# Two blocks of a network on one core: filler matmuls in TensorE's waits, and the values of two dilated heads in one step

## The reference

```
aff = softmax(h @ w_router);  vals, idx = top_k(aff^T, 32)      # per expert
hid = silu(xs @ w_gate) * (xs @ w_up);  y = (hid @ w_down) * vals
out[idx] += y
```

```
for (window, dilation) in ((128, 1), (512, 4), (2048, 16)):     # three configurations of every dilated head
    o, lse = attention(q, k, v, offsets 0, dilation, 2*dilation, ... up to window)
out = sum(softmax(lse over the three) * o)
```

## Time and profile before

| | |
|---|---|
| three timed executions | 1688.23, 1692.89, 1694.29 us |
| their median | 1692.89 us |
| the profiled execution, its own time | 1685.1 us |
| its span | 1683.2 us |
| mean granted clock of TensorE | 0.921 |
| TensorE busy | 1423.9 us (85%) |
| weight loads of TensorE | 796.6 us (47%) |
| VectorE busy | 509.1 us (30%) |
| ScalarE busy | 314.7 us (19%) |
| mean rate of the DMA | 293 GB/s |

### The profile page before, as it was taken

The page is one execution under the profiler, slowest core; times in us unless marked ns, Lnnn a source line. Parts: engine busy times, 40 slices in busy tenths (PEclk is TensorE's granted clock), DMA queues, the critical chain, the costliest instruction groups (busy, mean ns, idle before and its releaser), DMA issues.

```text
span 1683.2 us, 19028 instructions
## 1 busy us (share of the span) xinstructions
PE 1423.9 (85%) x7528; PEld 796.6 (47%) x7528; DVE 509.1 (30%) x1140; ACT 314.7 (19%) x659; POOL 0.2 (0%) x4
## 2 busy tenths in 40 slices
PE   6999998765766656579999899987899998999877
PEld 3665777321221211146768643432467677434323
DVE  5125362200111100014674422221336644222213
ACT  2422111100000000012322312210222223122102
POOL 0000000000000000000000000000000000000000
PEclk9999799888887878789999899999999999999989
DMA  9465219999999999991521389999715123799994
GB/s 383 167 228 200 100 50 390 382 428 428 427 428 428 428 428 427 426 415 53 200 100 51 150 338 412 412 417 411 322 50 200 64 87 150 311 415 408 416 413 161
DMA packets 56386, 492.62 MB, mean 293 GB/s; under 512 B 6240, under 2 KB 6624, under 8 KB 25952
## 3 DMA queue, kind: packets, MB, share of 16 engines
q1 hardware_dynamic: 56144, 491.15, 71.4%
q10 hardware_dynamic: 144, 0.13, 0.0%
HBM read 490.21 MB, written 1.05 MB: 292 GB/s over the span
## 4 chain that ended last, share of the span: by engine, by line
PE 60%; DMA 25%; DVE 6%; SPq 6%; issue 2%; ACT 1%; DVEq 0%; ACTq 0%
DMA A<-ring_d 21%; PE PS L635 20%; PE PS L1455 7%; SPq L3059 6%; PE PS L1484 4%; PE PS L959 4%; DMA A<-ranked_d 4%; PE PS L1319 3%; PE PS L640 3%; PE PS L1435 2%; PE PS L1501 2%; PE PS L1308 1%; PE PS L1145 1%; PE PS L1272 1%; PE PS L700 1%
## 5 line engine op out<-in xcount | busy, mean ns | idle before, releaser
L635 PE MATMUL PS<-A 128*128 128x256 f32 (+6 forms) x1720 | 413.7, 399 | 5.0 <-DMA A<-ring_d 2.7
L959 PE MATMUL PS<-A 128*32 128x512 f32 x1536 | 236.6, 753 | 143.4 <-DMA A<-ring_d 143.1
L635 PEld LDWEIGHTS PS<-A 128*128 128x128 f32 (+1 forms) x1720 | 308.5, 197 | 100.8 <-issue 58.4
L1455 PE MATMUL PS<-A 128*64 128x512 f32 (+1 forms) x1024 | 197.5, 635 | 23.7 <-DMA A<-ranked_d 23.6
L959 PEld LDWEIGHTS PS<-A 128*32 128x32 f32 x1536 | 52.2, 124 | 317.9 <-issue 239.7
L1455 PEld LDWEIGHTS PS<-A 128*64 128x64 f32 (+1 forms) x1024 | 58.5, 131 | 142.9 <-issue 141.0
L1975 DVE TENSOR_TENSOR A<-A,PS 128x512 f32<-128x512 f32 x8 | 5.5, 688 | 331.1 <-PE PS L959 331.1
L1484 PE MATMUL PS<-A 128*64 128x512 f32 (+1 forms) x512 | 94.9, 597 | 0.7 <-issue 0.7
L640 PE MATMUL PS<-A 128*128 128x128 f32 (+1 forms) x444 | 69.5, 289 | 29.2 <-DVE A L1975 7.1
L640 PEld LDWEIGHTS PS<-A 128*128 128x128 f32 (+1 forms) x444 | 53.5, 148 | 69.0 <-issue 39.2
L2426 DVE TENSOR_TENSOR A<-A,PS 128x256 f32<-128x256 f32 x26 | 11.0, 423 | 214.5 <-ACT A L2964 214.5
(11 more groups left out here) (352 smaller groups left out, 1259.6 us busy)
## 6 DMA issues: line engine op xcount, KB each, us to landing
A<-ring_d SPq DMA_DIRECT2D x156, 2048.0 KB, 23.3
A<-ranked_d SPq DMA_DIRECT2D x72, 1024.0 KB, 16.4
A<-ranked_d SPq DMA_DIRECT2D x144, 512.0 KB, 15.3
A<-ring_d SPq DMA_DIRECT2D x2, 1312.0 KB, 21.7
A<-ring_d SPq DMA_DIRECT2D x2, 1280.0 KB, 21.9
A<-p_d SPq DMA_DIRECT2D x1, 1232.0 KB, 21.9
A<-xT_d SPq DMA_DIRECT2D x1, 1024.0 KB, 5.6
A<-cT_d SPq DMA_DIRECT2D x1, 1024.0 KB, 12.0
```

What stands on the lines that cost most here:

```text
L635: ins = g.matmul(out, l, r, start=n == 0, stop=n == len(pairs) - 1)
L959: ins = g.matmul(ps[32 * e:32 * e + 32, :], rows_of(kk, e), wv[:, kk % 2, e, :], start=kk == 0, stop=kk == 7)
L1455: ins = g.matmul(ps[m * s:m * s + m, :], XS2[u % 2][:, kk, c:c + m], wv[:, kk % nk, s, :], start=kk == 0, stop=kk == 7)
```

## The change

It has two parts. A helper `keep_on(n, ...)` takes a PSUM bank and issues n matmuls of 128x128 by 256 columns on constants into it; nothing reads the result. By default its operands are the identity and the constants next to it. It is called at the places listed above: 8 ahead of the context's column sum, 10 ahead of `k(1, 0)`, 18 ahead of `aft`, 19 ahead of `post`, 4 and 6 ahead of the waits for the last two weight blocks of the first block's experts, 2 ahead of `fstd`, 2 ahead of `kx` in layer 0, and in both layers 17 ahead of `psx`, 12 at the end of the experts, ahead of the branch, and 12 ahead of `rb`. Each call takes a bank, so the rotation of the banks moves on by one there.

The second part computes the values of two dilated heads in one step. The step of the even head does nothing any more, and that of the odd head waits for the transposes of both and issues their products by turns, so that the two halves of the output rows alternate. In `head_steps`, which all engines follow, this step stands ahead of the normalization and the transposes of the unit before, rather than at the end of the turn.

```diff
@@ head_steps
         out += front
+        pair = t > 1 and units[t - 2][0] == "dil"
+        if pair and units[t - 2][1] % 2:
+            out.append(("pv", *units[t - 2]))
         if 0 < t <= len(units):
             out += [("nr", *units[t - 1]), ("tr", *units[t - 1])]
         out += behind
-        if t > 1:
+        if t > 1 and not pair:
             out.append(("pv", *units[t - 2]))
@@ tensor
+            def keep_on(n, *where, take=fresh, of=None):
+
+                ps = take("idle", *where)
+                for _ in range(n):
+                    ins = g.matmul(ps[:, 0:256], *(of or (ident, V(o1, 256))), start=True, stop=True)
+                ins.then_inc(*up("pe", "idle", *where))
             def csum():
+                keep_on(8, "csum", of=(ONES, p1("posc")))
                 column_sum(SQ, 8, ("csum",), (("csq", 0), ("csq", 1)))
             def k(s, j):
+                if (s, j) == (1, 0):
+                    keep_on(10, "k", of=(ONES, p1("posc")))
@@ four_experts
+                    if done == ("ye", 3, 1) and part > 1:
+                        keep_on((4, 6)[part - 2], "ye", part)
                     arrived(i)
+            keep_on(18, "aft")
             ps = fresh("aft")
+            keep_on(19, "post")
             ps = fresh("post")
+            keep_on(2, "fstd")
             ps = fresh("fstd")
@@ norm_pe
+            keep_on(12, "rb", l)
             for b in range(4):
@@ mixers_pe
             def kx():
                 load("A", "A", l)
+                if l == 0:
+                    keep_on(2, "kx")
+            def pv_of_two(u):
+
+                key = out_bank(l, "dil", u)
+                ps = fresh(*key)
+                g.wait_ge(*at("vc", l, 0, 1))
+                g.wait_ge(*at("vc", l, 1, 1))
+                two = [(heads_of("dil", x), PT[TURNED["tr", "dil", x][0]]) for x in (u - 1, u)]
+                for x in (u - 1, u):
+                    g.wait_ge(*at("pt", l, "dil", x))
+                for c, j, t0 in ((0, 0, 0), (1, 0, 128), (2, 1, 128)):
+                    for x in range(3):
+                        for heads, pt in two:
+                            _, _, r, value = heads[x]
+                            ins = g.matmul(ps[r, t0:t0 + 128], value(j), pt[:, x, c * 128:(c + 1) * 128], start=c == 0 and x == 0, stop=False,
+                                           skip_group_check=True)
+                ins.then_inc(*full("pv", l, "dil", u))
+                note("pe", "full", "pv", l, "dil", u - 1)
             def pv(strand, u):
+                if strand == "dil":
+                    return pv_of_two(u)
+            keep_on(17, "psx", l)
             ps = fresh("psx", l)
@@ experts_pe
+            keep_on(12, "flag", l, take=high)
             note("pe", "e_end", l, "pe")
```

More of the change, by code:

```diff
@@ L1063, in tensor @@
             for l in range(2):
-                mixers_pe(g, l, fresh, weights, arrived, finished, group, turn, column_sum, across, full)
-                last_sum = experts_pe(g, l, weights, arrived, finished, group, turn, full)
+                mixers_pe(g, l, fresh, weights, arrived, finished, group, turn, column_sum, across, full, keep_on)
+                last_sum = experts_pe(g, l, weights, arrived, finished, group, turn, full, keep_on)
                 overflow_pe(g, l, group, turn)
@@ L1069, in tensor, with norm_pe @@
                 banks.i = 4
-                norm_pe(g, l, fresh, turn, full)
+                norm_pe(g, l, fresh, turn, full, keep_on)
                 note("pe", "layer_end", l, "pe")
-        def norm_pe(g, l, fresh, turn, full):
+        def norm_pe(g, l, fresh, turn, full, keep_on):
             def last_group(b):
@@ L1111, in group_share, with mixers_pe @@
             return ins
-        def mixers_pe(g, l, fresh, weights, arrived, finished, group, turn, column_sum, across, full):
+        def mixers_pe(g, l, fresh, weights, arrived, finished, group, turn, column_sum, across, full, keep_on):
             sig.stage = f"m{l}"
@@ L1289, in tr @@
                 ins.then_inc(*full("tr", l, strand, u))
+            def pv_of_two(u):
[14 more added lines that the diff above has]
+                note("pe", "full", "pv", l, "dil", u - 1)
             def pv(strand, u):
+                if strand == "dil":
+                    return pv_of_two(u)
                 key = out_bank(l, strand, u)
[L1293 to L1296, removed]
+                fresh(*key)
+                banks.hold(*key)
                 ps, pt = bank(*key), PT[TURNED["tr", strand, u][0]]
@@ L1306, in pv @@
                     for x, (_, _, r, value) in enumerate(heads):
-                        begin = c == 0 and (x == 0 or strand != "dil")
-                        ins = g.matmul(ps[r, t0:t0 + 128], value(j), pt[:, x, c * 128:(c + 1) * 128], start=begin, stop=False, skip_group_check=True)
+                        ins = g.matmul(ps[r, t0:t0 + 128], value(j), pt[:, x, c * 128:(c + 1) * 128], start=c == 0, stop=False, skip_group_check=True)
                 ins.then_inc(*full("pv", l, strand, u))
-                if strand != "dil" or u % 2:
-                    banks.release(*key)
+                banks.release(*key)
             def output(b, k0, k1):
@@ L1386, in mixers_pe, with experts_pe @@
             group(ps[:, 0:32], [(ONES, SEL2[:, ti, 4:36]) for ti in range(2)]).then_inc(*full("cnt", l))
-        def experts_pe(g, l, weights, arrived, finished, group, turn, full):
+        def experts_pe(g, l, weights, arrived, finished, group, turn, full, keep_on):
             sig.stage = f"e{l}"
```

## The result

The changed kernel takes 1702.93 us (median of six runs, 1701.05 to 1704.73); the kernel before took 1690.2 us in the six runs beside it. The ratio is 1.0086, 95% interval 1.0061 to 1.011: slower by 14.5 us, inside the range, 3.9 us above the predicted time. So the sign and the range held, but the sum had found only about half of the difference between the two profiled executions.

A forecast was written before the change was run, and what follows sets the result against it. TensorE was taken to set the pace in some stages and full DMA in others. Terms summed to +8.3 us, 1685.1 becoming 1693.4 in the profiled execution; forecast 1699, 6 above the median 1692.89, range 1685 to 1708.

The forecast's parts named there:

- The rival in which ordinary executions win by the filler: Cold stretches are longer in ordinary executions than the profiled one; filler wins half back: 1690 to 1694; chance 0.15.
- The price of one matmul without a reader: All filler places: 0.434 us a call at full clock, 0.80 at half; calls beyond the wait delay what follows.
- the routing of the first block: 18 and 19 calls in waits of 5.29 and 5.47 us: overruns, less a warmer gather, sum +3.0 us.
- The rival in which the filler fits into the waits: Everywhere: a call costs about 0.28 us, overruns vanish, -11.6 us, 1679; chance 0.13.
- the one in which the clock does not stay up: Behind the filler, overruns and cold work both stay: about 17 us more, 1716; chance 0.05.
- Before the last transposes: End of each layer: twelve calls overrun a 3.14 us wait, sixteen transposes speed up; together +2.0 us.
- Before the overflow branch: Twelve calls after the experts: layer 0 -0.2, layer 1 loses 4.0; +3.8 taken, +10.4 kept for the range.
- the rival with it: The overflow branch waits for the filler, or the key projection stays cold: adds 6.6 or 2.9 us; chance 0.22.
- The values of two dilated heads at a time: Dilated heads in both layers: cheaper paired products, but new order delays transposes and scores; +3.8 us over two layers.
- End of the first block's experts: Filler at the last weight waits, final norm and layer 0 key projection: sum -4.0 us, other bound -1.1.
- the last sixteen instructions, -1.3: End of the first block's experts: partly cold 3.24 us become an estimated 1.9 at full clock, -1.3 us.
- Setup: Eight calls before the context's column sum cost 0; ten before the first k give -0.2 us.

The follow-up runs named there:

- the best version: Kernel before plus fitted filler counts, dilated pairs in their old place, and layer 1 weights issued only after layer 0's last down projection: 1662.24 us, ratio 0.9832.

## Why the prediction was right, and where it was not

**The number.** The sign came from overruns that were priced rightly. That 1702.93 falls within the forecast's own 1694 to 1704 is in part luck: the sum of +8.3 left 13.7 us of cost out, 3.7 us of cold stretches went the other way, and the profiled execution of before, 1685.1 us, is shorter than the six timed beside the changed kernel (1687.71 to 1694.29), so that their medians are 12.7 us apart and not 17.6. The rival in which ordinary executions win by the filler (1690 to 1694) is out.

**The price of one matmul without a reader** was right: 36 instructions in 8.02 us are 0.446 us a call, 24 in 5.45 are 0.454. With it went the routing of the first block (+3.0, and the gather at 3.81 for 3.74 foreseen), psx in both layers, the branch of layer 1 (+4.1), and the last transposes. The rival in which the filler fits into the waits is out, and so is the one in which the clock does not stay up: the key projection of layer 0 takes 3.69 us for 6.50.

**Before the last transposes.** Sixteen transposes behind the filler took 1.91 us in both layers, 1.95 having been estimated, and the projection behind them 3.62. The Trainium skill (TensorE: Matmul & The Clock Gate, Part 4: PE-mode transpose) says that transposes don't count as work for the clock. As the prediction read it, they would have been slow again; the trace shows sixteen of them at full clock right behind dense matmuls, and no run here tests a longer row of them.

**Before the overflow branch** is the step that failed. It said that in layer 0 the twelve calls would be 1.3 us late and get 1.5 back (-0.2); they cost 7.2. The error was to take the gap of 3.98 us as time that filler covers. In both layers alike the last sum comes 4.1 us later with the 5.2 us of filler, so only 1.1 of it was covered; and the packet of q8 ahead of the last sum begins about 4 us later too. In layer 0 the last sum then gives its 1.4 us back, as foreseen, but a second gap of 4.03 us for 0.73 and cold rows behind it (3.43 for 1.97) make it 7.2. The bound that I kept, a branch begun only after the filler, comes near in size (+10.4 for 7.2 and 4.1), and so does the rival with it; but it has each layer pay the whole 5.2 and knows no second gap.

What the runs show on the gap itself: it is 3.98 to 4.44 us in the eight kernels without filler there whose DMA was full, and 1.42 and 1.48 in the two whose DMA was empty. That the second gap comes from the 24 instructions that now stand in the way is shown (it goes with them, and it goes with the stream). In the two kernels that have it, the projection starts 1.36 and 1.54 us after the end of a packet of q8. That TensorE waits for just these packets is argued from such times. I had the two gaps of the earlier trace rows before me, 3.98 and 1.24, and did not put them beside the DMA share at the same moments (the number before the last in the stretches of 2 us of the kernel before, layer 0 and layer 1):

```profile
1198.00:1200.00 2.00, 0.81 (x1) 0.50 (x2) 0.00 (x0) 0.00 (x0) 0.00 (x0) 0.66 0.97 397
...
1662.00:1664.00 2.00, 0.83 (x2) 0.49 (x3) 0.69 (x1) 0.00 (x0) 0.00 (x0) 1.00 0.05 12
```

The DMA is full in the one and at 0.05 in the other.

**The values of two dilated heads at a time** had its mechanism right and one term missing. The waits came as worked out: 1.76 us for 1.9 ahead of the transposes, 1.31 for 1.3 ahead of the last pair, and in times of before the scores of dil 2 at 901.05 for 901.7. The waits alone cost 1.0 us a layer, less than the 1.9 predicted, partly because a pair takes 2.19 us and not 2.4. The Trainium skill (TensorE: Matmul & The Clock Gate, Part 3: Packing small matmuls) has matmuls in different column groups start about 4 ns apart. The prediction's estimate from it was 1.95 us; the measured 2.19 lies between the row and this estimate. This term was the second mis-sized one. What was missing is the clock behind two waits of 1.76 and 2.26 us: +3.3 a layer, as the run with filler in them shows. I had counted the clock as something that the change gives back, and never as something that its own new waits take.

**End of the first block's experts.** The key projection gave its 2.8 us. The term "the last sixteen instructions, -1.3" came to nothing: the sixteen take 1.92 us for 3.24, but they start 1.6 us later, since TensorE came to the filler of 2.86 us only at 733.96, 1.5 us of that through a cold stretch at 715.74 far ahead.

**Setup** was right in what it spoke of (k 0.25 earlier). The 2.6 us around it, and 1.1 in the experts of layer 1, are cold stretches at other places than before. They went the right way for the kernel after and hid a quarter of the missing cost in this one execution. Whether the other timed executions have them is not known, and what moves them was not tried.

## What to carry to other kernels

Fill a wait up to a small remainder, never past its end: 17 to 19 calls in the long waits and 12 ahead of the branch lost 10.3 us; 10 or 11, and none ahead of the branch, won 17.4. Some 11 of these 27.7 us are the branch alone. When an order is changed, price each wait that it opens twice, once for its length and once for the clock behind it, and prefer the place where the moved work still covers another engine's chain. A gap put down to "issue" is to be held against the share of the DMA at that moment: where the weight stream was full here, a pause of the stream helped, and work for the array did not.

## What was not expected of the hardware

Instructions come through DMA queues of their own, and under a full stream of weights they come late: at one branch the gap ahead of the last sum is 3.98 to 4.44 us under a DMA share near 1.0, 1.42 and 1.48 without, and 0.29 behind filler without. Pausing the stream there is worth 5.1 us to the kernel before, and it is in the best version, which beats the kernel before by 28.4 us.

After two waits of 1.76 and 2.26 us with 1.7 us of work between them the clock fell, in both layers, and it fell when the engine was back at work. With the same waits shortened to 0.27 and 0.53 us by matmuls that nobody reads, it stays at 2.4 GHz, at no cost in time. Short remainders are not always enough: behind 0.45, 0.72 and 1.0 us in the routing of the first block the gather ran cold in all three kernels with fitted filler.
